# Hybrid decoder block on one core: the last two units of the gate product by halves of 256 tokens, with the final norm and the stores of one half beside the other, and the work of three earlier stages reordered

## What is computed

```
h = x + concat(pool_mixer, attention) @ w_o
q = rmsnorm(h) @ peer_wq                          # 8 heads, two halves of 128 each
sc = q . sub_keys ; top_v, top_i = top_k(sc, 16)  # per head and half
cand = top_v[0][:, None] + top_v[1][None, :]      # best 16 pairs -> expert ids
gate = softmax(best_v)
h = h + sum_k gate_k * gelu(xn . u[expert_k]) * v[expert_k]
g = sigmoid(rmsnorm(h) @ ple_w_gate)              # 2048 x 2048: "gate product"
h = h + g * (p @ ple_w_proj)                      # 256 x 2048: "projection"
return rmsnorm(h)                                 # "final norm"
```

## Time and profile before

| what | us |
|---|---|
| median of 3 runs | 3002.37 |
| lowest, highest run | 3000.9, 3005.94 |
| the profiled execution, its own time | 2999.24 |
| its span | 2997.4 |
| TensorE busy in it | 2948.0 |
| VectorE busy in it | 2461.5 |

### The profile page before, as it was taken

The page is one execution under the profiler, slowest core; times in us unless marked ns, Lnnn a source line. Parts: engine busy times, 40 slices in busy tenths (PEclk is TensorE's granted clock), DMA queues, the critical chain, the costliest instruction groups (busy, mean ns, idle before and its releaser), DMA issues.

```text
span 2997.4 us, 45381 instructions
## 1 busy us (share of the span) xinstructions
PE 2948.0 (98%) x17318; PEld 2747.6 (92%) x17318; DVE 2461.5 (82%) x3652; ACT 1054.5 (35%) x1429; POOL 795.8 (27%) x519
## 2 busy tenths in 40 slices
PE   9999999999999999999999999999999999999997
PEld 7777778898889999999999999999999999999786
DVE  7544444489999969999999999999999999998544
ACT  5224332232224653333333333333333333334422
POOL 0120000037776202222222233333333333430000
PEclk9999999999999999999999999999999999999998
DMA  4242222345567789999999999999999999993222
GB/s 169 92 158 99 84 72 96 112 125 145 136 153 210 277 293 361 345 362 384 367 381 361 370 383 372 381 348 379 369 368 373 369 372 362 380 368 145 85 98 98
DMA packets 206628, 779.49 MB, mean 260 GB/s; under 512 B 50512, under 2 KB 99920, under 8 KB 132176
## 3 DMA queue, kind: packets, MB, share of 16 engines
q1 hardware_dynamic: 133920, 413.90, 37.9%
q0 software_dynamic: 67680, 358.71, 33.0%
q10 hardware_dynamic: 4944, 5.81, 0.5%
HBM read 745.22 MB, written 33.10 MB: 260 GB/s over the span
## 4 chain that ended last, share of the span: by engine, by line
PE 80%; DVE 12%; issue 3%; DMA 3%; SPq 1%; ACT 1%; DVEq 0%; ACTq 0%
PE bank L648 25%; PE bank L649 24%; PE bank L650 24%; DVE w_lo L1581 1%; DVE w_lo L1594 1%; PE bank L739 1%; SPq L606 1%; PE bank L941 1%; DMA raw_whole<-in_u_t 1%; PE bank L762 1%; PE bank L740 1%; DMA raw_b_whole<-in_u_t 1%; DVE row L1975 1%; DMA raw_whole<-in_v_t 1%; DVE top_row L1935 1%
## 5 line engine op out<-in xcount | busy, mean ns | idle before, releaser
L648 PE MATMUL bank<-x_hi,w_hi 128*128 128x342 f32 (+1 forms) x2880 | 997.2, 346 | 16.1 <-DVE w_lo L1581 9.5
L649 PE MATMUL bank<-x_lo,w_hi 128*128 128x342 f32 (+1 forms) x2880 | 994.3, 345 | 0.0
L650 PE MATMUL bank<-x_hi,w_lo 128*128 128x342 f32 (+1 forms) x2880 | 987.6, 343 | 0.0
L648 PE MATMUL bank<-a_hi,w_hi 128*128 128x342 f32 x2048 | 652.5, 319 | 3.4 <-DVE a_lo L2076 2.3
L650 PE MATMUL bank<-a_hi,w_lo 128*128 128x342 f32 x2048 | 652.1, 318 | 0.0
L649 PE MATMUL bank<-a_lo,w_hi 128*128 128x342 f32 x2048 | 649.7, 317 | 0.0
L648 PEld LDWEIGHTS bank<-x_hi,w_hi 128*128 128x128 f32 x2880 | 545.4, 189 | 60.6 <-DVE w_lo L1581 6.7
L649 PEld LDWEIGHTS bank<-x_lo,w_hi 128*128 128x128 f32 x2880 | 544.1, 189 | 38.2 <-issue 1.2
L650 PEld LDWEIGHTS bank<-x_hi,w_lo 128*128 128x128 f32 x2880 | 543.9, 189 | 38.1
L648 PEld LDWEIGHTS bank<-a_hi,w_hi 128*128 128x128 f32 x2048 | 387.1, 189 | 7.0 <-issue 3.4
L649 PEld LDWEIGHTS bank<-a_lo,w_hi 128*128 128x128 f32 x2048 | 387.2, 189 | 0.0
(11 more groups left out here) (265 smaller groups left out, 3182.2 us busy)
## 6 DMA issues: line engine op xcount, KB each, us to landing
raw_whole<-in_v_t SPq DMA_DIRECT2D x62, 1024.0 KB, 8.2
raw_b_whole<-in_v_t SPq DMA_DIRECT2D x62, 1024.0 KB, 8.0
raw_b_whole<-in_u_t SPq DMA_DIRECT2D x46, 1024.0 KB, 9.3
raw_whole<-in_u_t SPq DMA_DIRECT2D x46, 1024.0 KB, 9.2
raw_whole<-in_u_t SPq DMA_DIRECT2D x72, 512.0 KB, 3.8
beside<-gate_matrix SPq DMA_DIRECT2D x31, 704.0 KB, 14.9
raw_whole<-in_w_o SPq DMA_DIRECT2D x32, 512.0 KB, 3.5
raw_whole<-in_w_q SPq DMA_DIRECT2D x32, 512.0 KB, 3.5
```

The costliest lines, as they stand in the source:

```text
L648: pe.matmul(out, w_hi[slot][:, blk, :], m_hi, start=first, stop=False)
L649: pe.matmul(out, w_hi[slot][:, blk, :], m_lo, start=False, stop=False)
L650: return pe.matmul(out, w_lo[slot][:, blk, :], m_hi, start=False, stop=last)
```

## The change

- Heads: the sum over 16 picks becomes two additions of halves (16 to 8, 8 to 4, for both index tiles in one instruction each) and a `tensor_reduce` over 4. `TOP` goes from 7 to 5 and `EARLY` from 8 to 10: the dots of the last two heads move into the one-hot stage, whose dots stand at sets 1, 5, 9, 13, 17, 25 and 26 instead of 1, 7, 15, 25 and 26.
- Projection: ScalarE's squares (`third_sq`) and VectorE's sums (`third_sum`) of blocks 4 to 15 are taken out of `third_hi` and `third_lo` and stand after and between the later copy-outs; the first four copies of ScalarE stand between the scaled copies.
- End: units 14 and 15 of the gate product run as four half units of 256 tokens: 14 and 15 for the first half of the tokens, then 14 and 15 for the second. The column sums of the first half's squares stand at the end of the third half unit, the spreading matmul in the middle of the fourth. VectorE's products of the final norm are 32 of 256 columns, of which the first half's stand before, between and after the steps of the second half; 13 DMAs store them.

```diff
-TOP = 7
-EARLY = 8
+TOP = 5
+EARLY = 10
...
+PARTS = [slice(0, T // 2), slice(T // 2, T)]
+HALF_BANK = {(DC - 2, 0): 0, (DC - 1, 0): 1, (DC - 2, 1): 4, (DC - 1, 1): 2}
+SPREAD_BANK = (5, 3)
+AHEAD = 7
...
+        picked_both = at("picked_both", one + 27 * K, [P, 2 * TC * TOPK, TOPK], BF16)
+        picked = [picked_both[:, TC * TOPK * i:TC * TOPK * (i + 1), :] for i in range(2)]
...
-            ends = (1, 2, 4, 6, 8, 10, 12, 14, 15, 16)
-            for a, b in zip((0,) + ends, ends):
-                sp.wait_ge(fin_ready, b)
-                sp.dma_start(out_t[:, a:b, :], proj[:, a:b, :]).then_inc(out_stored, 16)
-            sp.wait_ge(out_stored, 16 * len(ends))
+            ends = ((2, 5, 9, 13, 16), (2, 4, 6, 8, 10, 12, 14, 16))
+            for part in range(2):
+                for a, b in zip((0,) + ends[part], ends[part]):
+                    sp.wait_ge(fin_ready, DC * part + b)
+                    sp.dma_start(out_t[:, a:b, PARTS[part]], proj[:, a:b, PARTS[part]]).then_inc(out_stored, 16)
+            sp.wait_ge(out_stored, 16 * sum(len(e) for e in ends))
...
+            pe.wait_ge(act_proj_out, DC // 2)
...
+            def half_unit(n, part, quarter_done):
+                ts = PARTS[part]
+                unit(n + U_GATE, (n + U_GATE) % 2, bank[HALF_BANK[n, part]][:, ts], lambda b: x2_hi[:, b, ts],
+                     lambda b: x2_lo[:, b, ts], quarter_done=quarter_done)
...
+            def squares(part):
+                for q in range(2 * part, 2 * part + 2):
+                    for n in range(2):
+                        mm = pe.matmul(bank[7][:, 2 * q:2 * q + 2], sq_h[n][:, q * P:(q + 1) * P], ones[:, 0:2],
+                                       start=n == 0, stop=n == 1)
+                mm.then_inc(stat_sum, 1)
...
+            def spread(part):
+                for q in range(2 * part, 2 * part + 2):
+                    pe.wait_ge(diag_ready, q + 1)
+                    mm = pe.matmul(bank[SPREAD_BANK[part]][:, q * P:(q + 1) * P], ones[:, :], diag[:, q, :],
+                                   start=True, stop=True)
+                mm.then_inc(stat_sum, 1)
...
                 if quarter == 2:
-                    pe.wait_ge(acc_step, 3 * ACC - 1)
+                    pe.wait_ge(acc_step, 3 * ACC - 2)
...
+            def first_squares(quarter):
+                if quarter == 3:
+                    pe.wait_ge(half_sq, 2)
+                    squares(0)
+
+            def first_spread(quarter):
+                if quarter == 1:
+                    spread(0)
             pe.wait_ge(gate_pre, DC - 3)
-            unit_x2(U_GATE + DC - 2, U_GATE % 2, 0)
+            half_unit(DC - 2, 0, None)
             pe.wait_ge(gate_pre, DC - 2)
-            unit_x2(U_GATE + DC - 1, (U_GATE + 1) % 2, 1, quarter_done=sums_ahead)
-            pe.wait_ge(end_sq, DC)
-            column_sums(bank[7], sq_h[0])
-            for q in range(TC):
-                pe.wait_ge(diag_ready, q + 1)
-                mm = pe.matmul(bank[5][:, q * P:(q + 1) * P], ones[:, :], diag[:, q, :], start=True, stop=True)
-            mm.then_inc(stat_sum, 1)
+            half_unit(DC - 1, 0, sums_ahead)
+            half_unit(DC - 2, 1, first_squares)
+            half_unit(DC - 1, 1, first_spread)
+            pe.wait_ge(half_sq, 4)
+            squares(1)
+            spread(1)
...
+
+            def third_sq(c):
                 if c >= 2:
                     act.wait_ge(acc_step, ACC + c)
                 act.activation(sq_h[c % 2][:, :], h[:, c, :], ACT.Square).then_inc(h3_sq, 1)
...
                     if last and q == 3:
+                        for c in range(4, 8):
+                            third_hi(c)
                         hi(U_PROJ, U_PROJ % 2, ahead=N_AHEAD)
...
-                    if last and q:
-                        for c in range(2 * q - 2, 2 * q if q < 3 else DC):
+                    if last and 0 < q < 3:
+                        for c in range(2 * q - 2, 2 * q):
                             third_hi(c)
-                            if c == 9:
-                                hi(U_PROJ + 1, (U_PROJ + 1) % 2, ahead=N_AHEAD)
+                            third_sq(c)
...
+            third_hi(8)
+            third_hi(9)
+            hi(U_PROJ + 1, (U_PROJ + 1) % 2, ahead=N_AHEAD)
             for n in range(0, DC, 2):
                 if n == 8:
                     hi(U_GATE, U_GATE % 2, ahead=N_AHEAD)
                 act.wait_ge(proj_done, n + 1 - n // 8)
                 act.activation(proj[:, n, :], bank[n % 8][:, :], ACT.Copy).then_inc(act_proj_out, 1)
+                if n < 6:
+                    third_hi(n + 10)
+                    third_hi(n + 11)
+                elif n >= 8:
+                    third_sq(n - 4)
+                    third_sq(n - 3)
+            for c in range(12, DC):
+                third_sq(c)
             hi(U_GATE + 1, (U_GATE + 1) % 2, ahead=N_AHEAD)
             std(4, rinv)
...
-            with act.Fori(0, (DC - 2) // 2) as i:
+            with act.Fori(0, (DC - 4) // 2) as i:
                 gate_out(2 * i + 1, 1)
                 gate_out(2 * i + 2, 0)
-            gate_out(DC - 1, 1, more=False)
-            act.wait_ge(col_var, 1)
-            act.activation(row_sum[:, :], row_sum[:, :], ACT.Sqrt).then_inc(col_std, 1)
+            gate_out(DC - 3, 1)
+            hi(U_GATE + DC - 1, (U_GATE + 1) % 2, ahead=N_AHEAD)
...
+            def half_sigmoid(n, part):
+                ts = PARTS[part]
+                act.wait_ge(gate_pre, n + 1 + 2 * part)
+                act.activation(g_sig[:, ts], g_pre[:, ts], ACT.Sigmoid).then_inc(gate_sig, 1)
+
+            for part in range(2):
+                half_sigmoid(DC - 2, part)
+                half_sigmoid(DC - 1, part)
+                act.wait_ge(col_var, part + 1)
+                act.activation(row_sum[:, 2 * part:2 * part + 2], row_sum[:, 2 * part:2 * part + 2], ACT.Sqrt)\
+                   .then_inc(col_std, 1)
...
+
+                def fold(n):
+                    return dve.tensor_tensor(picked_both[:, :, 0:n], picked_both[:, :, 0:n], picked_both[:, :, n:2 * n],
+                                             ALU.add)
+
+                step(fold(TOPK // 2))
+                fold(TOPK // 4)
...
+                    dve.tensor_reduce(chosen(p), picked[p][:, :, 0:TOPK // 4].rearrange("p (t k) m -> p t k m", t=TC),
...
-            with dve.Fori(2, PH) as i:
+            with dve.Fori(2, TOP + 2) as i:
+                choose_head(i)
+            for i in range(TOP + 2, PH):
                 choose_head(i)
...
-            top_dot(TOP - 1)
...
-                for k, at_set in ((3, 1), (4, 7), (5, 15), (6, N_OH - 2), (7, N_OH - 1)):
+                for k, at_set in ((3, 1), (4, 5), (5, 9), (6, 13), (7, 17), (8, N_OH - 2), (9, N_OH - 1)):
                     if at_set == q:
                         early_dot(k)
...
+                            if c < 4:
+                                third_sum(c)
...
+            def third_sum(c):
...
             for c in range(6, DC):
                 third_lo(c)
+                if c == 9:
+                    lo(U_PROJ + 1, (U_PROJ + 1) % 2)
                 if c in (9, 11, 13):
                     proj_out(c - 8)
-                if c == 9:
-                    lo(U_PROJ + 1, (U_PROJ + 1) % 2)
             proj_out(7)
             lo(U_GATE, U_GATE % 2)
             for n in range(9, DC, 2):
                 proj_out(n)
+                third_sum(n - 5)
+                third_sum(n - 4)
+            for c in range(12, DC):
+                third_sum(c)
             lo(U_GATE + 1, (U_GATE + 1) % 2)
...
-            with dve.Fori(0, (DC - 2) // 2) as i:
+            with dve.Fori(0, (DC - 4) // 2) as i:
                 gate_out(2 * i + 1, 1)
                 gate_out(2 * i + 2, 0)
+            gate_out(DC - 3, 1)
+            lo(U_GATE + DC - 1, (U_GATE + 1) % 2)
...
+            def half_out(n, part):
+
+                ts, done = PARTS[part], n + 1 + 2 * part
+                dve.wait_ge(weights_used, U_GATE + done)
+                dve.tensor_tensor(g_pre[:, ts], bank[HALF_BANK[n, part]][:, ts], rinv[:, ts], ALU.mult).then_inc(gate_pre, 1)
+                dve.wait_ge(gate_sig, done)
+                dve.tensor_tensor(g_mul[:, ts], g_sig[:, ts], proj[:, n, ts], ALU.mult).then_inc(gate_mul, 1)
+                dve.wait_ge(gate_mul, done)
+                dve.tensor_tensor(h[:, n, ts], h[:, n, ts], g_mul[:, ts], ALU.add).then_inc(h_end, 1)
+                dve.wait_ge(h_end, done)
+                dve.tensor_tensor(sq_h[n % 2][:, ts], h[:, n, ts], h[:, n, ts], ALU.mult).then_inc(half_sq, 1)
...
+            def final(part, c):
+                ts = PARTS[part]
+                dve.scalar_tensor_tensor(proj[:, c, ts], h[:, c, ts],
+                                         gain[:, G_FIN - C_GAIN + c:G_FIN - C_GAIN + c + 1],
+                                         bank[SPREAD_BANK[part]][:, ts], ALU.mult, ALU.mult).then_inc(fin_ready, 1)
...
+            def inverse_of(part):
```

(46 more changed lines are left out.)

12 lines of the change are left out of this document (2 added, 10 removed).

## The result

The changed kernel took 2986.11 us (median of 6 runs, 2984.12 to 2987.75), the one before 3002.28 us (median of 6, 2999.26 to 3005.94). The ratio is 0.9947, with a 95% interval from 0.9935 to 0.9959: 16 us less. The profiled execution took 2986.3 us, its span is 2984.5.

A forecast was written before the change was run, and what follows sets the result against it. TensorE, busy in 98% of the span, was taken as the bound, so only its gaps, slow clock and end could give time. Heads 6.8 + one-hot 0 + projection 9.4 + end 3.1 = 19.3 us: 3002.4 to 2983, range 2975 to 2991.

The forecast's parts named there:

- G: Projection: the copy-outs stay behind something else, the wait for DMA of the second weights; 7 us remain, 2992; chance 0.03.
- Dearer and added matmuls: End: 256-column matmuls in place of 512, plus column-sum and spreading matmuls, make the last product end 3.1 us later.
- The tail: End: VectorE's work behind the last product shrinks from 19.2 to 13.3 us, 5.9 less.
- The wait for the last store: End: the wait for the last store taken as 2.8 instead of 3.1 us.
- C: End: the 256-column matmul is bound by its load at 0.155 to 0.19 us; +7 to +13 us, 2990 to 2996; chance 0.08.
- F: Half units: a 256-column product is handled like a plain f32 one; +60 us, 3043; chance 0.04.
- D: The end gives nothing, through 1 KB stores or a clock drop before the last sums; 2987; chance 0.06.
- E: End: the sigmoid's table load costs 2.66 us in all, not 1.28; block 15's steps 1.3 us late, 2984.4; chance 0.03.
- A: Heads: the additions run at the slow rate, so the heads give 1.3 us instead of 6.8; 2988.5; chance 0.12.
- The slow clock behind it: Heads: of nearly 3 us lost in the slow stretch behind the longest gap, 0.9 us counted as won, between 0 and 2.8.
- the one-hot stage: Two dots added, 4.6 us of VectorE against 5.2 us free; booked at 0, 4.5 us if the cover is gone.
- rival B: One-hot stage: the added dots stall TensorE, up to 4.5 us back, 2987.5; chance 0.06.

The follow-up runs named there:

- e_proj: The kernel before with the projection's part of the change alone: 2993.69 us (median of 12), ratio 0.9969.
- e_heads: The kernel before with the heads' part of the change alone: 2997.22 us (median of 12), ratio 0.9974.
- h_light: The kernel before with the heads' part alone, and only half of each gathered row fetched in the expert stage: 2985.57 us (median of 4).
- a_light: The changed kernel with only half of each gathered row fetched in the expert stage: 2971.54 us (median of 4).
- e_end: The kernel before with the end's part of the change alone: 3001.08 us (median of 12), ratio 0.9992.
- a_noheads: The changed kernel with the heads' part undone, so projection and end alone: 2987.04 us (median of 8), ratio 0.9963.
- b_light: The kernel before with only half of each gathered row fetched in the expert stage: 2990.68 us (median of 5).
- v_dot: The changed kernel with two early dots later, the third at set 0 and the fourth at set 2: 2986.36 us (median of 6), ratio 0.9954.
- a_delay6: The changed kernel with six idle VectorE products (13.8 us) in the last head: 2997.37 us (median of 12), ratio 0.9987.

## Why the prediction was right or wrong

**Right in sum, and in part by luck.** Forecast 2983 (19.3 us less), measured 2986.11 and 2984.02 (16.2 and 17.1 less by medians). The projection and the end (12.5 forecast, 12.9 measured) came out by their own steps. For the heads two steps were off by over 4 us each in the first pair of profiles, with opposite signs.

**The projection: right.** Forecast 9.4 us, measured 9.49 between the two first profiles and 9.5 in `e_proj` alone. Gap and low clock both went, as the steps said, so G is out. The first copy-out came at 2771.32, forecast 2773.3.

**The end: right, term by term.** Dearer and added matmuls: from the start of the gate product to block 15's last result it is 2968.53 - 2789.06 = 179.5 us, before 2975.09 - 2798.55 = 176.5; 2.9 us, forecast 3.1. The tail: 13.1 us, forecast 13.3. The wait for the last store: 2984.5 - 2981.62 = 2.9, forecast 2.8. Sum 3.4, forecast 3.1. The spacing is 0.120 us as worked out from 512 columns, so C and F are out. The 0.27 us that the prediction takes off a VectorE step with half the columns, for which no row stood, came out too: 0.69 us became 0.42 (the row at 2968.53). The 1 KB runs of the stores cost nothing behind VectorE (D out), but the DMA engines are busy for 0.97 of that stretch; whether a faster VectorE would have met them was not tried. For E, the table load takes 1.28 us and the sigmoid starts at 2963.94, 0.01 us behind it. The Trainium skill (ScalarE: Activation LUTs, "What ACT_TABLE_LOAD costs") adds a drain of about the same size; the trace does not agree, here as in the earlier trace rows.

**The heads: mechanism right, sizes off.** On VectorE the instructions cost what the sum said: additions and small reductions take 1.17 + 0.65 us (the 0.65 is 878.24 - 877.58, where the next instruction starts), forecast 1.8, so A is out. But VectorE won more than these. Its low part is 6.28 us earlier when the loop ends (879.24 against 885.52), forecast 4.7, and 8.26 earlier ahead of the longest gap (910.83 against 919.09), forecast 5.9. The trip shown is 3.49 us shorter, forecast 0.5 + 2.3; the other 0.7 is in shorter waits between its small steps. TensorE's gap ends the same 8.26 us earlier. The slow clock behind it, booked at 0.9, gave back 2.7: its matmuls start 0.285 us apart (16 of them from 921.17 to 925.73), and not 0.26, for which the prediction divided the stretch by its count. So TensorE was 11.0 us ahead, forecast 6.8. The waits for low parts are 5.0 us, forecast 4 to 5.

What failed comes after it: I booked the 6.8 us as reaching the end, with the one-hot stage as the only thing in between, at 0.

First, that stage took 4.6 us in the first pair, 11.0 at its first set less 6.3 at its last. In the mean of the five profiles with the heads' part as changed (the changed kernel twice, `e_heads`, `h_light`, `a_light`) and the five without it (before, `e_proj`, `e_end`, `a_noheads`, `b_light`), the first set starts at 938.7 and 947.3 us, the last at 1062.8 and 1069.0: 8.6 us of lead become 6.2. The first gathers (1084.8 to 1090.3, mean 1088.4, and 1093.8 to 1095.7, mean 1094.7) show the same 6.3. In the first pair 2.7 us go by 962.54 (970.79 before), at the waits for one-hot tiles, and 1.9 later, where TensorE has two gaps of 0.36 and 0.33 us; the rest is in waits too short for the view. That is the place and, in this pair, the size of rival B, which had 4.5 us and a chance of 0.06. The forecast stood because the heads had given 4.2 us more than it said, and that is luck. Whether the added dots are the cause stays open: `v_dot`, with two dots moved, takes 122.9 us from the first set to the last, the changed kernel 125.0 and 125.6, but `a_light`, with the dots where the changed kernel has them, 121.2, and the five without the heads' part 120.4 to 123.4.

Second, the expert stage, which I had not looked at: its 610 MB run at a DMA share of 0.95 to 0.99. With half rows 5.1 us of the heads arrive. With whole rows the whole change gives 16.2 to 17.1 us, of which projection and end, 12.9 to 13.0, are read from the traces; 3 to 4 are left for the heads, 3 less than forecast. My reading, that an earlier TensorE is there sooner than its weights, is argued and not shown, and one profile speaks against it. From the first gather to the last, the four whole-row profiles without the heads' part take 1601.0 to 1603.7 us, the six with it 1604.9 to 1611.3. `a_delay6` is among the six, with 1609.9, though it enters the stage 7.4 us later than the kernel before and has no lead to lose; it waits there for low parts like the others, longer than the one 4.2 us of before:

```profile
PE bank L657 <- DVE w_lo L1657: 7.3, 6, 2.2
```

So the heads' part may lengthen this stage by something other than its lead. No run separates the two.

**What stays open** is this share. `e_heads` alone gave 7.8 us (4.2 to 11.4), the comparison with `a_noheads` anything from 1 to 8, and in the profiled executions nothing arrives: the projection starts at 2766.5 us in the mean of the four whole-row kernels without the heads' part (2764.7 to 2768.1) and at 2766.4 in the four with it (2763.3 to 2767.6). As the time from the projection to the end repeats (the column "rest"), the projection of a median run can be estimated: its time less 1.8 us, less "rest". That gives 2768.0 to 2771.5 for the four whole-row kernels without the heads' part (the kernel before by its first six runs) and 2764.8 to 2767.4 for the four with it, 4.2 us apart in the mean. The profiled executions do not lie alike in their runs: without the heads' part they are 0 to 6.5 us below the medians of their kernels, with it from 1.7 below to 3.0 above. I have no trace of the other executions. That some 3 to 4 us of the 6.3 arrive fits all, but the size is an estimate and its cause is not shown.

**The range** of 2975 to 2991 was built with a spread between runs of 2 to 3 us. Other chips showed 19 us for the kernel before (2995.8 to 3014.8) and 8 for the changed one (2978.5 to 2986.9 in six). The median stayed inside; a single run of the changed kernel could not have been told from a forecast 4 us off.

## What to carry to other kernels

Before a gain is carried from an early stage to the end, walk through every stage behind it and ask what paces it: here a stage with the DMA engines at 0.97 gave back part of a lead although TensorE looked 99.9% busy in the profile before. The cheapest test of it is to halve the transfers' bytes with everything else the same, and to see whether the stalls go. The changes behind that stage were summed from the rows to a few tenths of a microsecond; the one ahead of it was not. And follow the lead through the trace at work that both kernels share: a sum that comes out can hide two errors of opposite sign, here 4.2 and 4.6 us.

## What the runs showed of the hardware

- The time from the projection's first matmul to the end repeats to 0.1 us over executions and chips (217.1 to 217.2 in eight profiles), and with the old projection and end to 0.5 (230.2 to 230.7 in four). The stage from the first gather to the last takes 1601 to 1611 with whole rows (DMA share 0.95 to 0.99) and 1592.6 to 1594.7 with half rows (0.75 to 0.81), so the scatter of this kernel is made ahead of the projection.
- A bf16 addition of slices of 8 elements (1024 results, both index tiles in one instruction) takes as long as a product of 1024 with a broadcast operand, 0.69 us each in the mean of 8 and of 16; the one of slices of 4 (512 results) takes 0.45.
- Matmuls of 256 columns of this type start 0.120 us apart, of 512 columns 0.226: that is 0.414 ns a column and 0.014 us of each that does not shrink with the width.
- Stores in runs of 1 KB moved 326 GB/s at a DMA share of 0.97, those of 2 KB and more 395 at 0.99: by these two stretches the shorter runs keep the DMA engines busy a fifth longer per byte (an estimate: 326 / 0.97 against 395 / 0.99). VectorE made 128 KB per 0.40 us, 329 GB/s, so it was just hidden.
- A gap of TensorE of 1.27 us left the granted clock at 1.00, one of 2.47 us at 1090 us did not (0.79 over the 8 us around it). The one of 3.32 us before had brought it to 0.50.
